# One stage with the tokens on the partitions for the last combine, residual add, final norm and store

## What is computed

```python
def rmsnorm(x, g=None):
    xf = x.astype(jnp.float32)
    y = xf * lax.rsqrt(jnp.mean(xf * xf, axis=-1, keepdims=True) + NORM_EPS)
    if g is not None:
        y = y * g.astype(jnp.float32)
    return y.astype(x.dtype)
...
        xc = xc + mod_c[5][:, None, :] * moe_ffn(hc, ...)
        xl = xl + mod_l[5][:, None, :] * moe_ffn(hl, ...)
    y_prompt = rmsnorm(xc, final_norm_g)
    y_sample = rmsnorm(xl, final_norm_g)
```

## Time and profile before

| | |
|---|---|
| median of 3 runs | 2395.74 us (2388.3 to 2395.95) |
| span of the profiled execution | 2395.5 us |
| time of the profiled execution outside its span | none is recorded beside the span, so the span is its time |
| mean granted TensorE clock | 0.930 |
| TensorE, VectorE, ScalarE busy | 2090.6, 1268.6, 1007.9 us |
| first gather of the last combine issued | 2332.27 us |
| last instruction of VectorE ends | 2390.80 + 0.69 = 2391.49 us |

### The profile page before, as it was taken

One profiled execution on the slowest core, in us unless ns is written; L12 is line 12 of the kernel. 1 busy time (PEld: TensorE's weight loads), 2 busy tenths in 40 slices (PEclk: granted clock), 3 DMA queues, 4 the chain that ended last, 5 costly groups with the idle time before them and its releaser, 6 DMA issues. The chain is left out here.

```text
span 2395.5 us, 25968 instructions
## 1 busy us (share of the span) xinstructions
PE 2090.6 (87%) x8680; PEld 1434.7 (60%) x8680; DVE 1268.6 (53%) x1786; ACT 1007.9 (42%) x1387; POOL 112.0 (5%) x129
## 2 busy tenths in 40 slices
PE   5988899999649999946999999999999938999974
PEld 2434454554338788736756865875675526878853
DVE  5971432333459999944322422323242247999965
ACT  5762212122348888723211221222121126888853
POOL 0000000000010000011000100100010010000001
PEclk8998997999869999968999999999999968999996
DMA  9968000100569999652211220221210168999933
GB/s 357 387 233 329 22 28 9 36 18 0 211 239 393 398 399 398 250 183 96 79 44 53 70 88 18 71 83 56 70 35 18 55 231 293 399 399 398 399 128 125
DMA packets 181319, 424.90 MB, mean 177 GB/s; under 512 B 10621, under 2 KB 22426, under 8 KB 181274
## 3 DMA queue, kind: packets, MB, share of 16 engines
q1 hardware_dynamic: 164912, 365.52, 41.5%
q0 software_dynamic: 10944, 39.85, 4.5%
q10 hardware_dynamic: 5418, 18.96, 2.0%
HBM read 369.09 MB, written 55.21 MB: 177 GB/s over the span
## 5 line engine op out<-in xcount | busy, mean ns | idle before, releaser
L1790 DVE TENSOR_TENSOR moe_w_lo<-weight_ring,moe_w_hi 128x1024 fp32r<-128x1024 f32 x432 | 521.1, 1223 | 84.8 <-ACT moe_w_hi L1721 71.9
L1721 ACT ACTIVATE moe_w_hi<-weight_ring 128x1024 fp32r<-128x1024 f32 x432 | 456.4, 1061 | 194.8 <-PE ps L1653 126.0
L1251 DVE TENSOR_TENSOR ret_w_lo<-weight_ring,ret_w_hi 128x512 fp32r<-128x512 f32 x128 | 96.0, 750 | 285.9 <-ACT ret_w_hi L1187 285.9
L1653 PE MATMUL ps<-moe_w_hi,moe_rows_t_hi 128*128 128x512 f32 x576 | 233.2, 405 | 5.0 <-DVE moe_rows_t_lo L1795 4.7
L1653 PE MATMUL ps<-moe_w_hi,moe_rows_t_lo 128*128 128x512 f32 x576 | 227.1, 394 | 0.0
L1653 PE MATMUL ps<-moe_w_lo,moe_rows_t_hi 128*128 128x512 f32 x576 | 227.0, 394 | 0.0
L1187 ACT ACTIVATE ret_w_hi<-weight_ring 128x512 fp32r<-128x512 f32 x128 | 80.6, 632 | 309.2 <-PE ps L1064 309.2
L1064 PE MATMUL ps<-ret_w_hi,h_hi 128*128 128x512 f32 x480 | 194.1, 404 | 3.5 <-ACT weight_ring L1191 2.1
L1064 PE MATMUL ps<-ret_w_lo,h_hi 128*128 128x512 f32 x480 | 189.7, 395 | 0.0
L1064 PE MATMUL ps<-ret_w_hi,h_lo 128*128 128x512 f32 x480 | 189.7, 395 | 0.0
L1653 PEld LDWEIGHTS ps<-moe_w_hi,moe_rows_t_hi 128*128 128x128 f32 x576 | 109.6, 190 | 27.6 <-DVE moe_rows_t_lo L1795 5.5
(11 more groups left out here) (288 smaller groups left out, 3256.3 us busy)
## 6 DMA issues: line engine op xcount, KB each, us to landing
weight_ring<-in_moe_w_gate SPq DMA_DIRECT2D x36, 2048.0 KB, 12.3
weight_ring<-in_moe_w_up SPq DMA_DIRECT2D x36, 2048.0 KB, 13.4
weight_ring<-in_moe_w_down SPq DMA_DIRECT2D x36, 2048.0 KB, 12.3
weight_ring<-in_ada_w SPq DMA_DIRECT2D x24, 2048.0 KB, 17.0
weight_ring<-in_ret_w_in SPq DMA_DIRECT2D x12, 2048.0 KB, 8.5
h_normed<-rows_in POOLq DMA_DIRECT2D x36, 512.0 KB, 7.0
rows_out<-h_normed ACTq DMA_DIRECT2D x36, 512.0 KB, 6.2
rows_in<-zero_rows SPq DMA_DIRECT2D x26, 512.0 KB, 7.2
```

The costliest lines, as they stand in the source:

```text
L1251: dve.tensor_tensor(wlo[:, n % BUF, :], win[s][:, k, :], whi[:, n % BUF, :].bitcast(F32), ALU.subtract).then_inc(w_lo, 1)
L1653: mm = pe.matmul(out, lhs, rhs, start=(first and x == 0), stop=(last and x == 2))
L1721: nc.scalar.activation(whi[:, x, :], part(u, w + x), ACT.Identity).then_inc(w_hi, 1)
L1790: dve.tensor_tensor(wlo[:, x, :], part(blk[1], w + x), whi[:, x, :].bitcast(F32), ALU.subtract).then_inc(w_lo, 1)
```

## The change

`combine` stays for the first layer. For the last layer, `combine`, the last `norm` and `write_out` are replaced by one block, `combine_out`, which keeps the tokens on the partitions. For each tile of 128 tokens TensorE transposes `c.x` into two PSUM banks and leaves the accumulation open (`turn`). The weighted sum of the two expert rows is multiplied by the gate, which must now be a row of 1024 on all partitions: VectorE builds eight diagonal matrices for each of the two gates, and TensorE multiplies them by ones into four PSUM banks. Then TensorE adds the gated rows to the transposed `c.x` in PSUM, by a product with the identity. ScalarE squares that sum and accumulates over the free dimension into one value for each token, takes the root; VectorE takes the reciprocal of a 128x1 column and scales the rows, out of PSUM, by it and by the gain (a row loaded once for all partitions). SyncE stores. Two tiles have their banks at one time. In `setup` the gain's columns and the zeros go.

```diff
@@ -130,8 +130,6 @@
         self.amp = sb("norm_amplitude", [P, DEPTH, 2, KD, 2])
         self.cols_a = sb("norm_gain_and_ada_bias", [P, P])
         self.cols_b = sb("other_columns", [P, 32])
-        self.zero2 = sb("no_shift", [P, KD, 2])
-        self.fin2 = sb("final_gain", [P, KD, 2])
...
@@ -187,7 +185,6 @@
             @block.gpsimd
             def _(pool):
                 pool.memset(c.eps[:, :], EPS).then_inc(memsets, 1)
-                pool.memset(c.zero2[:, :, :], 0.0).then_inc(memsets, 1)
                 pool.memset(rows_b[:, :], 0.0).then_inc(memsets, 1)
...
-                act.wait_ge(memsets, 3)
-                for r, n in ((0, "c_ctx"), (8, "c"), (16, "final_norm_g"), (24, "mla_q_norm_g"), (27, "mla_kv_norm_g")):
+                act.wait_ge(memsets, 2)
+                for r, n in ((0, "c_ctx"), (8, "c"), (24, "mla_q_norm_g"), (27, "mla_kv_norm_g")):
...
@@ -248,13 +245,10 @@
                 dve.tensor_copy(c.cols_a[:, :], ps[:, 0, 0:P]).then_inc(taken_v, 1)
                 dve.wait_ge(turned, 2)
                 dve.tensor_copy(c.cols_b[:, :], ps[:, 1, 0:32]).then_inc(taken_v, 1)
-                dve.wait_ge(taken_v, 2)
-                dve.tensor_copy(c.fin2[:, :, 0], c.cols_b[:, 16:24]).then_inc(taken_v, 1)
                 for g in range(0, 2 * NT, 2):
                     dve.wait_ge(turned, g + 3)
                     dve.tensor_copy(c.x[:, 0:4, (g // 2) * P:(g // 2 + 1) * P],
                                     ps[:, 2 + g % 6, :].rearrange("p (k n) -> p k n", k=4)).then_inc(taken_v, 1)
-                dve.tensor_copy(c.fin2[:, :, 1], c.cols_b[:, 16:24]).then_inc(taken_v, 1)
...
@@ -1898,44 +1892,119 @@
                                                      op0=ALU.mult, op1=ALU.add).then_inc(added, 1)
 
 
-def write_out(c):
+def combine_out(c, layer):
 
     nc, ops, ps = c.nc, c.ops, c.ps
+    gate = c.mod[:, layer, 40:48, :]
+    GATES, TILES = (0, 2), (4, 6)
     with ExitStack() as st:
-        rows = st.enter_context(nc.sbuf_tensor("out_rows", [P, NT, D], F32))
-        turned, taken, taken_v, out_s = sems(nc, st, "out", ["turned", "act", "dve", "stored"])
+        y = st.enter_context(nc.sbuf_tensor("fin_rows", [P, NT, TOPK, D], F32))
+        diag = st.enter_context(nc.sbuf_tensor("fin_diagonals", [P, 2, KD, P], F32))
+        gain = st.enter_context(nc.sbuf_tensor("fin_gain_row", [P, D], F32))
+        junk = st.enter_context(nc.sbuf_tensor("fin_squares", [P, D], F32))
+        ss = st.enter_context(nc.sbuf_tensor("fin_sumsq", [P, NT], F32))
+        got = sems(nc, st, "fin", [f"got{t}" for t in range(NT)])
+        (gain_in, diagonal, gates_made, turned, weighed, summed, gated, added, squared, rooted, inverted, normed,
+         out_s) = sems(nc, st, "fin", ["gain", "diagonal", "gates", "turned", "weighed", "summed", "gated", "added", "squared",
+                                       "rooted", "inverted", "normed", "stored"])
+
+        def acc(t):
+            return ps[:, TILES[t % 2]:TILES[t % 2] + 2, :].rearrange("p a n -> p (a n)")
+
         with nc.Block(no_gpsimd_drain=True) as block:
+            @block.gpsimd
+            def _(pool):
+                for t in range(NT):
+                    for k in range(TOPK):
+                        pool.indirect_dma_start(y[:, t, k, :], None, c.ys,
+                                                bass.IndirectOffsetOnAxis(c.dest[:, k, t:t + 1], 0)).then_inc(got[t], 16)
+
+            @block.sync
+            def _(sp):
+                sp.dma_start(gain[:, :], ops["final_norm_g"].rearrange("(a n) -> a n", a=1).broadcast_to([P, D])).then_inc(gain_in, 16)
+                for t in range(NT):
+                    sp.wait_ge(normed, t + 1)
+                    dst = ops["y_prompt"][0] if t == 0 else ops["y_sample"][0, (t - 1) * P:t * P]
+                    sp.dma_start(dst, y[:, t, 1, :]).then_inc(out_s, 16)
+                sp.wait_ge(out_s, 16 * NT)
+
             @block.tensor
             def _(pe):
-                for g in range(2 * NT):
-                    if g >= 8:
-                        pe.wait_ge(taken, (g - 8) // 2 + 1)
-                        pe.wait_ge(taken_v, (g - 8) // 2 + 1)
-                    for k in range(4):
-                        mm = pe.transpose(ps[:, g % 8, k * P:(k + 1) * P],
-                                          c.h[:, 4 * (g % 2) + k, (g // 2) * P:(g // 2 + 1) * P], c.base["ident"])
+                def turn(t):
+                    for k in range(KD):
+                        mm = pe.matmul(ps[:, TILES[t % 2] + k // 4, (k % 4) * P:(k % 4 + 1) * P], c.x[:, k, t * P:(t + 1) * P],
+                                       c.base["ident"], start=(k % 4 == 0), stop=False, is_transpose=True, skip_group_check=True)
                     mm.then_inc(turned, 1)
+
+                turn(0)
+                turn(1)
+                for j in range(2):
+                    pe.wait_ge(diagonal, j + 1)
+                    for k in range(KD):
+                        mm = pe.matmul(ps[:, GATES[j] + k // 4, (k % 4) * P:(k % 4 + 1) * P], c.base["ones"], diag[:, j, k, :],
+                                       start=True, stop=True)
+                    mm.then_inc(gates_made, 1)
+                for t in range(NT):
+                    pe.wait_ge(gated, t + 1)
+                    for b in range(2):
+                        mm = pe.matmul(ps[:, TILES[t % 2] + b, :], c.base["ident"], y[:, t, 0, b * 512:(b + 1) * 512],
+                                       start=False, stop=True, skip_group_check=True)
+                    mm.then_inc(added, 1)
+                    if 1 <= t < NT - 1:
+                        pe.wait_ge(normed, t)
+                        turn(t + 1)
 
             @block.scalar
             def _(act):
-                for g in range(0, 2 * NT, 2):
-                    act.wait_ge(turned, g + 1)
-                    nc.scalar.copy(rows[:, g // 2, 0:512], ps[:, g % 8, :]).then_inc(taken, 1)
+                def weigh(t):
+                    act.wait_ge(got[t], 16 * TOPK)
+                    nc.scalar.activation(y[:, t, 0, :], y[:, t, 0, :], ACT.Identity, scale=c.w12[:, 0, t:t + 1]).then_inc(weighed, 1)
+
+                weigh(0)
+                weigh(1)
+                for t in range(NT):
+                    act.wait_ge(added, t + 1)
+                    if t:
+                        act.wait_ge(squared, t)
+                    nc.scalar.activation(junk[:, :], acc(t), ACT.Square, accum_out=ss[:, t:t + 1]).then_inc(squared, 1)
+                    act.wait_ge(squared, t + 1)
+                    nc.scalar.activation(ss[:, t:t + 1], ss[:, t:t + 1], ACT.Sqrt, bias=c.eps[:, :], scale=1.0 / D).then_inc(rooted, 1)
+                    if t + 2 < NT:
+                        weigh(t + 2)
 
             @block.vector
             def _(dve):
-                for g in range(1, 2 * NT, 2):
-                    dve.wait_ge(turned, g + 1)
-                    dve.tensor_copy(rows[:, g // 2, 512:1024], ps[:, g % 8, :]).then_inc(taken_v, 1)
-
-            @block.sync
-            def _(sp):
-                for t in range(NT):
-                    sp.wait_ge(taken, t + 1)
-                    sp.wait_ge(taken_v, t + 1)
-                    dst = ops["y_prompt"][0] if t == 0 else ops["y_sample"][0, (t - 1) * P:t * P]
-                    sp.dma_start(dst, rows[:, t, :]).then_inc(out_s, 16)
-                sp.wait_ge(out_s, 16 * NT)
+                for j in range(2):
+                    dve.tensor_tensor(diag[:, j, :, :], c.base["ident"].unsqueeze(1).to_broadcast([P, KD, P]),
+                                      gate[:, :, j:j + 1].to_broadcast([P, KD, P]), ALU.mult).then_inc(diagonal, 1)
+
+                def add_up(t):
+                    j = 0 if t == 0 else 1
+                    dve.wait_ge(weighed, t + 1)
+                    dve.scalar_tensor_tensor(out=y[:, t, 0, :], in0=y[:, t, 1, :], scalar=c.w12[:, 1, t:t + 1],
+                                             in1=y[:, t, 0, :], op0=ALU.mult, op1=ALU.add).then_inc(summed, 1)
+                    dve.wait_ge(summed, t + 1)
+                    dve.wait_ge(gates_made, j + 1)
+                    dve.tensor_tensor(y[:, t, 0, :], y[:, t, 0, :], ps[:, GATES[j]:GATES[j] + 2, :].rearrange("p a n -> p (a n)"),
+                                      ALU.mult).then_inc(gated, 1)
+
+                def norm_rows(t):
+                    dve.wait_ge(rooted, t + 1)
+                    dve.reciprocal(ss[:, t:t + 1], ss[:, t:t + 1]).then_inc(inverted, 1)
+                    dve.wait_ge(inverted, t + 1)
+                    if t == 0:
+                        dve.wait_ge(gain_in, 16)
+                    dve.scalar_tensor_tensor(out=y[:, t, 1, :], in0=acc(t), scalar=ss[:, t:t + 1], in1=gain[:, :],
+                                             op0=ALU.mult, op1=ALU.mult).then_inc(normed, 1)
+
+                for t in range(NT + 1):
+                    if t < NT:
+                        add_up(t)
+                    if t:
```

(7 more changed lines are left out.)

## The result

The changed kernel took 2362.89 us (median of four runs, 2360.18 to 2372.03), the kernel before 2395.84 beside it (2388.3 to 2397.07): a ratio of 0.9869, 95% interval 0.9831 to 0.9906. So it is faster by about 1%, and the medians give the size of the gain to some 10 us only; why is part of what follows. A run's time is 1.6 to 2.8 us longer than the span of its profile, mostly 1.7 (2361.8 beside a span of 2360.1).

The account below looks back on a forecast made before the run. No engine bounds the whole 63.2 us tail of three consecutive stages; running them per tile ends the span at 2371.3, 24.2 us off 2395.5; off the median 2371.5, with half a microsecond for waits 2372.0; range 2363 to 2379.

Parts of the forecast that it names:

- The structure: New last-layer stage: VectorE's add_up(t+1) then norm_rows(t) sets the pace; first two adds at slow clock, the rest fast; chance 0.60.
- The gathers' delay: Start of the new stage: VectorE's two diagonal products hold up the first gather, 1.4 us, bounds 0 and 2.0.
- VectorE's round: Per tile in the new stage: add_up 2.54 and norm_rows 1.5, so 4.04 us if nothing else is late.
- The store's tail: From the last scaled row to the end of the span: 4.0 us, as in the write-out before.
- The table load: Before the first tile's square root on ScalarE: one load of 1.28 us, with no drain counted.
- The gate products: TensorE's opening: sixteen fp32 products for the gate rows, 6.9 us at the slow clock, hidden behind the gathers.
- Nothing ahead of the tail moves: Stages ahead of the change stay as they are; the smaller setup counts 0.
- The half microsecond of reserve: Added for waits between engines priced at nothing: 2371.5 becomes 2372.0.
- Span and time: Whole kernel: profiled span 2395.5 and median run time 2395.74 taken as the same to 0.01%.
- Rival 1: New stage: slow clock throughout makes TensorE the bound, 5.6 us a tile, 2376; chance 0.24, shared with a dearer start.
- Rivals 2, 3 and 4: VectorE delays gathers 3 us: 2373; root's table reloads each tile: 2375.8, chance 0.04; gain row late: 2377, chance 0.04.
- rival 4: Gain row's load takes 21 us, holding up tile 0's scaling: 2377, chance 0.04; slower than before, 0.03.

## Why the prediction held, and what was off in it

Times after the last store's issue, as predicted (its times less 2328.48) and measured (less 2319.11):

| step | predicted | measured |
|---|---|---|
| tile 0 weighed from | 11.8 | 10.9 |
| tile 0 gated | 15.5 | 14.6 |
| tile 0 added, square begins | 19.2 | 18.5 |
| tile 0 rooted | 21.8 | 21.2 |
| tile 0 normed | 23.4 | 22.7 |
| tile 4 gated | 34.0 | 32.8 |
| tile 4 normed | 38.8 | 37.9 |
| end | 42.8 | 41.0 |

- **The structure** was right: VectorE's add_up and norm_rows as the round, two tiles in flight, one table load on tile 0's path, the first add slow, the second in part, and the rest fast, the gate rows hidden, the gain row never waited for. The fast rest was partly luck: in the second profile of the same program tile 2's add was slow as well (below).
- **The gathers' delay** was over-sized: 1.4 us priced, 0.4 measured at issue (1.43 against 1.01) and 0.5 at tile 0's weighing (10.9 against 10.4 in the kernel before). The diagonals start 0.7 us ahead of the gather, and it gets in between the two, ending 0.9 us after the first. As the Trainium skill has it ("SBUF — State Buffer", SBUF: two separate sides), the lock is held for the whole instruction; the trace agrees with that too, since the gather ends at 2324.34, within the second product.
- **VectorE's round** 3.83 in place of 4.04: consecutive operations overlap by some 0.07 us. From tile 0's scaled row to tile 4's gating that makes 10.1 us in place of 10.6.
- **The store's tail** 3.1 in place of 4.0: I had taken it over from the write-out, where five stores were issued within 5 us. Here they are 3.6 us apart and more. That the crowd made the difference is likely and not tested.
- **The table load** cost 1.25 us, 1.28 priced. The Trainium skill's drain of 1.4 us behind it ("ScalarE: Activation LUTs", What ACT_TABLE_LOAD costs) isn't there: the load ends at 2339.99 and the root starts at 2340.01. The measurement goes before the page's figure.
- **The gate products** took 3.74 us, at the fast clock, where I had 6.9 for the slow one; hidden either way.
- **Nothing ahead of the tail moves** was the step on which the number 2372 rested, and it needs a word. In a single comparison it can fail by 9 us or more, since the time ahead has levels of its own. The first median, 2362.9, lies 9 us below 2372.0 for that reason, at the very bottom of the range of 2363 to 2379 and below the 2368 to 2373 that had the best chance. That the range reached so low was reserve for the spread of the runs, which I had seen as 7.6 us and not as levels 27 us apart. Over sixteen runs the changed kernel's median is 2369.7, 2.3 us below. The tail was over-sized by 1.8 us: 0.9 at the gathers, 0.9 at the store and 0.5 in the rounds, less 0.5 for steps a little dearer than priced. The half microsecond of reserve was not wanted. As a gain of the tail, 24.2 us predicted stands beside 24.4 to 27.1 measured.
- **Span and time** were set equal. In all later runs the time is 1.6 us or more above the span, so, if that holds for the kernel before as well, its profiled execution was one of about 2397 and not the median one. Since I took 24.2 us off the median, and not the end of the new stage as it stood, that cost nothing.
- **Rival 1** (TensorE the bound, slow clock) did not come in the rounds of the first profile, but a part of it did in the second execution of the changed kernel: tile 2's add

```profile
2347.47 1.76 PE L1938 MATMUL ps<-base_consts,x_resid 128*128 128x128 f32 x8 [1.96 <-DVE fin_rows L2000]
2349.92 3.78 PE L1953 MATMUL ps<-fin_rows,base_consts 128*128 128x512 f32 x4 [0.69 <-DVE fin_rows L1991]
```

  took 3.78 us and the tail 42.7. Which of the two comes, in the same program, the runs don't settle. I had given the choice no price between the two extremes. Rivals 2, 3 and 4 are excluded by the trace: of the gathers that tiles 0 to 2 wait for only the first is stretched, there is one table load, and no wait for the gain. The 21 us at which rival 4 priced a slow load of the gain row were far off, it landed 5.0 us after its issue:

```profile
fin_gain_row<-in_final_norm_g SPq DMA_DIRECT2D x1, 512.0 KB, 5.0
```

## What to carry to other kernels

When several stages over all tokens follow each other, price the merged stage by one tile's latency and by the round of the busiest engine. The gain hangs on the overlap, and is lost, here 21.8 of 26.0 us, if the order of one engine lets only one tile be in work. Look for what sits in the first tile's latency and could be done while nothing else can run: the table load cost nothing once a dummy activation called it up during a wait. And cut every profile at the last instruction ahead of the change before comparing two spans; of four runs three had drawn the low level of stages that no edit touched. Profile the same program more than once, too: the tail of the unedited stage itself spread over 2.7 us, more than the table load or the first adds are worth.

## What the runs showed of the hardware that I had not expected

- The attention stage runs at half TensorE's clock for stretches of some 30 to 34 us, once or three times in an execution, with TensorE busy for 90% of them and more (30.64 of 34 us at 0.52 above). With the place and number of these stretches go levels of the time ahead: 2318 to 2319, 2325 to 2328, 2347. No kernel and no chip is tied to one level (each of three chips met at least two); what chooses it is open.
- A gather held up by a VectorE operation with two SBUF inputs gets in behind that one operation, though the next one follows with no gap (2322.91 + 1.43 = 2324.34, in the middle of the second diagonal product, which ends at 2324.59).
- A little more work can be faster: fourteen products that nobody reads and two more passes of a gate product took some 1.7 us off the first profile's tail, beside the table load's 1.25, since the adds of tiles 0 and 1 took 1.98 us each at a granted clock of 1.00 (2.4 GHz) where the first had taken 3.8 at 0.50 (1.2 GHz). With the two passes alone the tail was only 0.6 us shorter than in the first profile, since the clock then fell one tile later.
- GpSimd takes 2.87 us to scale 128x1024 and 2.36 to add two such tiles, where VectorE does both in one operation of 1.28 us.
